# Two halves of 256 tokens in both down projections of the third feed-forward block

## The reference, cut to what matters

```
D_FF_2 = 2816

def swiglu(h, w_gu, w_dn):
    g, u = jnp.split(h @ w_gu, 2, axis=-1)
    return (jax.nn.silu(g) * u) @ w_dn
...
        h = rmsnorm_2(x, g_pre[l, 2]) * (1 + sc3) + sh3
        x = x + 0.5 * gt3 * rmsnorm_2(swiglu(h, w_gu2[l], w_dn2[l]), g_post[l, 2])
    return x
```

## Time and profile before

| | before |
|---|---|
| median of 3 runs | 2310.77 us |
| lowest and highest run | 2303.08 and 2311.32 us |
| span of the profiled execution, first to last instruction | 2309.7 us |
| median less that span (the profile lists no whole time for its execution) | 1.1 us |
| PE busy | 98% of the span |
| mean granted TensorE clock, 1 is full speed | 0.987 |

### The profile page before, as it was taken

How to read it: one execution, slowest core, us unless ns; L and a number is a source line. 1 busy time by engine, 2 the same in 40 slices (tenths; PEclk the granted TensorE clock), 3 DMA queues, 4 the chain that set the end, 5 groups by cost and what they waited for, 6 DMA issues and landing times.

```text
span 2309.7 us, 33182 instructions
## 1 busy us (share of the span) xinstructions
PE 2272.5 (98%) x10598; PEld 1871.6 (81%) x10598; DVE 992.4 (43%) x1647; ACT 898.9 (39%) x1624; POOL 1044.4 (45%) x800
## 2 busy tenths in 40 slices
PE   8999999999999999999999999999999999999997
PEld 7888888888888888888888878888677787888886
DVE  6899885526523314110014325555665555110112
ACT  4334663333322232332333354444665453332332
POOL 3455553444444443544445433333422354444444
PEclk9999999999999999999999999999999999999998
DMA  4333433337746532333333223333311432333331
GB/s 154 95 96 101 145 116 146 92 114 280 265 133 215 186 92 73 96 95 97 99 95 95 75 80 110 109 109 118 128 51 52 150 95 74 96 98 98 93 98 60
DMA packets 129483, 263.95 MB, mean 114 GB/s; under 512 B 14256, under 2 KB 14384, under 8 KB 128624
## 3 DMA queue, kind: packets, MB, share of 16 engines
q1 hardware_dynamic: 119520, 236.51, 33.7%
q10 hardware_dynamic: 9872, 26.25, 3.0%
HBM read 250.02 MB, written 12.58 MB: 114 GB/s over the span
## 4 chain that ended last, share of the span: by engine, by line
PE 89%; DVE 5%; issue 2%; ACT 2%; POOL 1%; DMA 0%; ACTq 0%; DVEq 0%; POOLq 0%
PE bank L1021 25%; PE bank L1023 25%; PE bank L1022 25%; PE bank L1290 2%; PE bank L1292 2%; PE bank L1291 2%; PE bank L1380 1%; PE bank L1343 1%; PE bank L1424 1%; POOL wlo L415 1%; PE bank L1446 1%; DVE bank L1695 1%; PE bank L1365 1%; PE bank L1193 1%; PE bank L1177 1%
## 5 line engine op out<-in xcount | busy, mean ns | idle before, releaser
L415 POOL TENSOR_TENSOR wlo<-raw,whi 128x512 fp32r<-128x512 f32 x750 | 989.3, 1326 | 1175.4 <-ACT whi L511 1174.7
L1021 PE MATMUL bank<-a_hi,whi 128*128 128x512 f32 x1928 | 762.0, 395 | 5.4 <-POOL wlo L415 2.1
L1023 PE MATMUL bank<-a_lo,whi 128*128 128x512 f32 x1928 | 751.0, 390 | 0.0
L1022 PE MATMUL bank<-a_hi,wlo 128*128 128x512 f32 x1928 | 750.3, 389 | 0.0
L511 ACT ACTIVATE whi<-raw 128x512 fp32r<-128x512 f32 x750 | 468.6, 627 | 685.0 <-PE bank L1023 612.7
L1021 PEld LDWEIGHTS bank<-a_hi,whi 128*128 128x128 f32 x1928 | 362.0, 188 | 87.2 <-issue 6.2
L1023 PEld LDWEIGHTS bank<-a_lo,whi 128*128 128x128 f32 x1928 | 361.9, 188 | 76.5
L1022 PEld LDWEIGHTS bank<-a_hi,wlo 128*128 128x128 f32 x1928 | 362.1, 188 | 75.5 <-issue 1.4
L1021 PE MATMUL bank<-b_hi,whi 128*128 128x512 f32 x852 | 336.0, 394 | 0.6 <-DVE b_lo L1833 0.3
L1023 PE MATMUL bank<-b_lo,whi 128*128 128x512 f32 x852 | 332.5, 390 | 0.0
L1022 PE MATMUL bank<-b_hi,wlo 128*128 128x512 f32 x852 | 332.5, 390 | 0.0
(11 more groups left out here) (275 smaller groups left out, 1815.8 us busy)
## 6 DMA issues: line engine op xcount, KB each, us to landing
raw<-d_stream SPq DMA_DIRECT2D x750, 256.0 KB, 2.6
G<-d_ada SPq DMA_DIRECT2D x72, 512.0 KB, 4.5
spill_rv<-tmp ACTq DMA_DIRECT2D x32, 256.0 KB, 2.1
G<-spill_rv ACTq DMA_DIRECT2D x8, 1024.0 KB, 8.2
G<-d_x ACTq DMA_DIRECT2D x4, 512.0 KB, 5.7
spill_ga<-sq ACTq DMA_DIRECT2D x8, 256.0 KB, 3.6
G<-spill_ga ACTq DMA_DIRECT2D x1, 2048.0 KB, 8.2
G<-d_x ACTq DMA_DIRECT2D x1, 2048.0 KB, 13.5
```

Source lines behind the costliest of these rows:

```text
L415: pool.tensor_tensor(wlo[:, s % SRING, :], raw[:, s % RING, :], whi[:, s % SRING, :].bitcast(F32), ALU.subtract).then_inc(lo_done, 1)
L1021: pe.matmul(out_ps, w_hi, hi[:, k, :], start=first and q == 0, stop=False)
L1022: pe.matmul(out_ps, w_lo, hi[:, k, :], start=False, stop=False)
L1023: mm = pe.matmul(out_ps, w_hi, lo[:, k, :], start=False, stop=last and q == len(ks) - 1)
```

## The change

Inside `panel`, for the names dn3a and dn3b alone, each k is given to a new helper, which takes the first 256 tokens of the operand tile and the bank with three products, and then the other 256 tokens with three more. The weight tiles, the operands, the sums and their order for each output element stay as they were. The flag that opens the bank is on the first product of the first half alone; the flag that closes it is on the last product of each half at the last k.

```diff
         @block.tensor
         def _(pe):
+            HALVES = (slice(0, T // 2), slice(T // 2, T))
+
+            def half_products(out_ps, w_hi, w_lo, hi, lo, first, last):
+
+                for n, c in enumerate(HALVES):
+                    o = out_ps[:, c]
+                    pe.matmul(o, w_hi, hi[:, c], start=first and n == 0, stop=False, skip_group_check=True)
+                    pe.matmul(o, w_lo, hi[:, c], start=False, stop=False, skip_group_check=True)
+                    mm = pe.matmul(o, w_hi, lo[:, c], start=False, stop=last, skip_group_check=True)
+                return mm
+
...
                     w_hi, w_lo = whi[:, p % SRING, c], wlo[:, p % SRING, c]
+                    if name in ("dn3a", "dn3b"):
+                        mm = half_products(out_ps, w_hi, w_lo, hi[:, k, :], lo[:, k, :], first and q == 0,
+                                           last and q == len(ks) - 1)
+                        continue
                     pe.matmul(out_ps, w_hi, hi[:, k, :], start=first and q == 0, stop=False)
```

## The result

The changed kernel takes 2316.18 us, the median of 10 runs (2313.77 to 2318.39). Ten runs of the kernel before, the three known ones among them, have a median of 2310.01 us (2303.08 to 2311.32). The ratio is 1.0032 with a 95% interval of 1.0022 to 1.0042: slower by 0.3%, well inside the 0.5% that was set as the bound of "same". The profiled execution took 2317.82 us with a span of 2316.0 us.

The account below looks back on a forecast made before the run. PE was taken to bound the kernel; 1056 half products at 120.0 ns add 7.0 us (3.8 in dn3a, 3.2 in dn3b) to 2310.8 us, giving 2317.8 us, +0.30%, with a range of 2308 to 2325 us.

Parts of the forecast that it names:

- PE sets the pace, one for one: In dn3a and dn3b PE never idles, so time added to a product is added to the end.
- The lower bound of 111 ns from loads in a row: Eight weight loads in a row stand 0.111 us apart, so half products cannot follow closer; at that distance, -2.4 us.
- Fixed surcharge, s = 120.0 ns: Distance between half products in dn3a and dn3b: 106.7 ns of columns plus 13.3 ns per product; +7.0 us, chance 0.54.
- The argument from plain float32: Plain float32 products at L1380 lengthen evenly with width, leaving 168 ns fixed; speaks for a surcharge by the instruction.
- The 8 ns that had no counterpart there: Float32r's fixed rest is about 8 ns above plain float32's; if by the column, s is 116 ns, +2.8 us.
- Rival B: Surcharge in dn3a and dn3b goes with columns in part or wholly: s 111 to 118 ns, -2 to +5 us; chance 0.22.
- Rival C: Loads or instruction issue set the half products' distance, deciding from 124.3 ns; at 130 ns +17.6 us; chance 0.17.
- Rival D: Each half product waits for a whole 188 ns load: s = 191 ns, +82 us (2393 us); chance 0.04.
- Rival E: Faster by over 0.5%, needing s under 102.3 ns, less than the columns alone take; chance 0.03.
- Small terms: In the down stages: half product 282 ns long, load 188 ns; last product ending about 0.1 us sooner, neglected.
- if the load's length grows: Named sign of being wrong: weight loads beside half products in the down stages becoming longer than 188 ns.
- The formula of the Trainium skill: Product distance at full clock of N / 2.4 + 2.5 ns: 109.2 ns per half product, sum +1.4 us.

Follow-up runs that it names:

- w128: Changed kernel with each operand tile of both down stages cut into four quarters of 128 columns instead of two halves: 2424.80 us, products 111.6 ns apart in dn3a.
- n192: Changed kernel with six products of 192 columns per operand tile in both down stages, last 128 tokens left out: products 111.6 ns apart in dn3a.
- n384: Changed kernel with three products of 384 columns per operand tile in both down stages, last 128 tokens left out: products 173.4 ns apart in dn3a.
- n320: Changed kernel with three products of 320 columns per operand tile in both down stages, last 192 tokens left out: products 146.6 ns apart in dn3a.
- c64n512: Changed kernel with uncut 512-column products and 64-column weight tiles in both down stages, half their output channels left out: products 230.0 ns apart in dn3a.

## Why the prediction was right

- **PE sets the pace, one for one.** Right. Idle time stayed 0.0, gu3b and the tail kept their lengths, and the 7.0 us of the two stages are the whole effect that the traces show. The medians differ by 6.2 us and the interval of the ratio reaches from 5 to 10 us. The time itself was forecast 1.6 us too high, about half of it because the three runs of before had a median of 2310.77 us and ten have 2310.01.
- **The lower bound of 111 ns from loads in a row.** Right: eight loads in a row gave the pace that w128 and n192 held for a whole stage, 111.6 ns.
- **Fixed surcharge, s = 120.0 ns.** The number was hit in both stages, and n384 and n320 show that the reason holds for full weight tiles. The argument from plain float32, whose length grows by its columns alone, pointed the right way, but whether another number format would carry over was open, as the prediction says. The 8 ns that had no counterpart there turned out fixed too (116 ns would have been the alternative). The prediction's wording, that the surcharge "belongs to the product", is too wide: with weight tiles of 64 columns it is another number at each width, and at the lower clock it is gone (last section).
- **Rival B** (surcharge by the column) fell with n384 and n320. **Rival C** (loads or issue take over) fell for 256 columns; the floor is real, but lies 8 ns lower, and what it costs is seen in w128. The queue delivered at 0.11 us a product for a whole stage, which the earlier trace rows had only for four. **Rival D** fell with the trace of the change: loads of 192 ns stand 120 ns apart, and in w128 111.6 ns apart. The sentence that the prediction cites from the Trainium skill, "TensorE: Matmul & The Clock Gate", section "The mechanism", on loads that overlap only with other row groups, does not hold for these products. The same section also has loads pulled ahead into a background weight buffer, which would fit; no run here shows whether it is that. **Rival E** did not come.
- **Small terms.** The half product is 283 ns long (282 expected). The load is 192 ns long where 188 was expected, and "if the load's length grows" was named as a sign of being wrong. It grew by 4 ns, but it doesn't set the 120 ns: in w128 and n192 loads of the same 192 ns stand 111.6 ns apart. The earlier end of the last product is there, 0.09 us.
- **The formula of the Trainium skill.** In the section that the prediction cites ("TensorE: Matmul & The Clock Gate", "Back-to-back issue gap"), N / 2.4 + 2.5 ns is given for a product taken by itself, without a budget for its load. It would have been 109.2 ns for the half products; the trace has 120.0.

## What to carry to other kernels

Read the cost of a product in a dense stretch from the distance of starts, not from its length, and split it into columns over clock and a rest. With full weight tiles at full clock the rest is paid once per product here, so cutting the streamed side in two costs it once more (here 13.3 ns for each of 528 extra products), and below some width the floor of the loads is all that counts (here 111.6 ns, reached between 256 and 192 columns). A row of loads that is busy near 100% doesn't by itself tell of a bound, since loads overlap each other (120.0 ns apart it was none, 111.6 ns apart it was); find their closest distance somewhere else in the same trace. When an effect is as small as the scatter of runs, apply the edit everywhere it can be applied and see whether it scales.

## What was not expected of the hardware

Narrower weight tiles made a stream of 512 columns slower: 226.7 ns with 128 weight columns, 230.0 with 64 and 231.7 with 32, with distances that no longer are all alike (224 to 236 ns in c64n512). At 256 streamed columns 64 weight columns made it faster, 113.3 against 120.0 ns.

The surcharge is also gone at the lower clock. A stretch of the kernel before in which the granted clock was 0.50, the 1.2 GHz level, by its window and its timeline:

```profile
359.00:362.00 3.00, 3.00 (x8) 2.32 (x8) 0.21 (x1) 0.00 (x0) 0.00 (x0) 0.50 0.84 326
```
```profile
358.73 0.63 PE L1022 MATMUL bank<-b_hi,wlo 128*128 128x512 f32 x1
...
361.72 0.63 PE L1023 MATMUL bank<-b_lo,whi 128*128 128x512 f32 x1
```

Seven distances in 2.99 us are 427 ns each, which is 512 / 1.2 to the nanosecond, with nothing on top. So the 13.3 ns are not work that each product adds to its columns under all conditions. It may be something that runs beside the stream and is covered when the stream is slow; no run tests that, and what it is stays open.

The floor of the loads moves with the clock too. In a stretch at a granted clock of 0.50, nineteen loads under products of one column, the last 0.33 us long, stand (4.15 - 0.33) / 18 = 0.212 us apart, about twice the 111 ns of the earlier trace rows:

```profile
12.43 4.15 PEld L1153 LDWEIGHTS bank<-ones,G 128*128 128x128 f32 x19
12.60:16.50 3.90, 3.90 (x20) 3.90 (x20) 1.39 (x6) 2.26 (x4) 3.34 (x3) 0.50 0.98 294
```
